# Two-layer hybrid decoder trunk: first weight tiles loaded in two pieces, angles computed early, k factors and k transposes moved, one output weight tile held back

## The reference, cut to what matters

```python
for layer in range(DEPTH):                       # DEPTH = 2
    if layer == 0:
        z = rms_norm(x, ab_norm_g) @ ab_w_in     # 512 pooling columns, 3 * 512 attention columns
        a = pool_mixer(z[..., :512], pool_w, pool_scale)
        b = diff_attention(z[..., 512:], cos, sin, ...)   # 4 heads, two softmax maps each, rotary on q and k
        x = x + concat([a, b]) @ ab_w_out
    else:
        z = rms_norm(x, ml_norm_g) @ ml_w_in     # q, k (short causal conv), v, output gate, gates
        h = rms_norm(mlstm_chunkwise(q, k, v, li, lf)) * sigmoid(o)   # 4 heads
        x = x + h @ ml_w_out
    x = x + conv_ffn(x, ...)                     # up 1024 -> 5632, causal conv, silu gate, down 2816 -> 1024
```

## Time and profile before

| | |
|---|---|
| median of 3 runs | 2274.3 us (2273.61 to 2274.34) |
| the profiled execution's own time | 2274.28 us |
| its span, first to last instruction | 2272.5 us |
| PE busy | 2261.0 us, 10747 matmuls |
| DVE, ACT, POOL busy | 1190.7, 572.2, 882.0 us |
| granted TensorE clock | 1.000 over the span |

### The profile page before, as it was taken

One profiled execution on the slowest core, in us unless ns is written; L12 is line 12 of the kernel. 1 busy time (PEld: TensorE's weight loads), 2 busy tenths in 40 slices (PEclk: granted clock), 3 DMA queues, 4 the chain that ended last, 5 costly groups with the idle time before them and its releaser, 6 DMA issues.

```text
span 2272.5 us, 27216 instructions
## 1 busy us (share of the span) xinstructions
PE 2261.0 (99%) x10747; PEld 1870.7 (82%) x10747; DVE 1190.7 (52%) x1176; ACT 572.2 (25%) x888; POOL 882.0 (39%) x395
## 2 busy tenths in 40 slices
PE   9999999999999999999999999999999999999999
PEld 7777778888888888888888898788888888888887
DVE  7776763464554555545644144444545555554554
ACT  5555441221111111111344333422111111111110
POOL 1212226444334433344643333275344433443342
PEclk9999999999999999999999999999999999999999
DMA  5111121111111111111321111031111111111111
GB/s 195 56 47 47 33 92 57 47 47 49 54 46 46 46 54 47 46 47 53 115 79 56 35 59 65 21 135 45 51 47 46 46 55 46 46 46 52 50 47 74
DMA packets 38721, 132.29 MB, mean 58 GB/s; under 512 B 4912, under 2 KB 6768, under 8 KB 38640
## 3 DMA queue, kind: packets, MB, share of 16 engines
q1 hardware_dynamic: 35760, 122.24, 16.7%
q10 hardware_dynamic: 2880, 8.91, 1.0%
HBM read 118.26 MB, written 8.68 MB: 56 GB/s over the span
## 4 chain that ended last, share of the span: by engine, by line
PE 95%; DVE 3%; issue 1%; ACT 0%; DMA 0%; SPq 0%; ACTq 0%; DVEq 0%
PE pj L1367 42%; PE dn L1387 17%; PE pj L347 15%; PE pj L325 6%; PE pj L1860 3%; PE dn L1438 3%; PE dn L686 1%; PE pj L712 1%; PE pj L1438 1%; PE pj L506 1%; PE pj L696 1%; PE dn L1998 1%; PE dn L2007 1%; PE dn L1886 1%; PE pj L1886 1%
## 5 line engine op out<-in xcount | busy, mean ns | idle before, releaser
L1661 POOL TENSOR_TENSOR w_hi<-w_raw,ones 128x1024 fp32r<-128x1024 f32 x186 | 356.0, 1914 | 1329.9 <-PE pj L1367 564.0
L1663 POOL TENSOR_TENSOR w_lo<-w_raw,w_hi 128x1024 fp32r<-128x1024 f32 x186 | 468.3, 2518 | 14.6
L1491 DVE SCALAR_TENSOR_TENSOR ffn_y<-ffn_h,params,ffn_y 128x1024 f32<-128x1024 f32 x176 | 323.6, 1838 | 117.6 <-ACT ffn_y L1499 109.0
L1499 ACT ACTIVATE ffn_y<-ffn_h,params 128x1024 f32<-128x1024 f32 x88 | 109.6, 1245 | 886.6 <-DVE ffn_h L1480 886.6
L1480 DVE TENSOR_TENSOR ffn_h<-pj,rms_bc 128x1024 f32<-128x1024 f32 x88 | 107.8, 1225 | 365.5 <-PE pj L1367 351.9
L1540 DVE TENSOR_TENSOR res<-dn,res 128x1024 f32<-128x1024 f32 x144 | 176.1, 1223 | 115.4 <-PE dn L1387 115.4
L1367 PE MATMUL pj<-xb_hi,w_hi 128*128 128x512 f32 x704 | 216.9, 389 | 0.0
L1367 PE MATMUL pj<-xa_hi,w_hi 128*128 128x512 f32 x704 | 216.9, 389 | 0.0
L1367 PE MATMUL pj<-xb_hi,w_lo 128*128 128x512 f32 x704 | 216.7, 389 | 0.0
L1367 PE MATMUL pj<-xa_hi,w_lo 128*128 128x512 f32 x704 | 216.7, 389 | 0.0
L1367 PE MATMUL pj<-xa_lo,w_hi 128*128 128x512 f32 x704 | 216.7, 389 | 0.0
(11 more groups left out here) (321 smaller groups left out, 3550.4 us busy)
## 6 DMA issues: line engine op xcount, KB each, us to landing
w_raw<-weights SPq DMA_DIRECT2D x189, 512.0 KB, 3.5
x_first<-x_t SPq DMA_DIRECT2D x8, 512.0 KB, 9.8
res<-x_t SPq DMA_DIRECT2D x8, 512.0 KB, 6.8
scratch<-res ACTq DMA_DIRECT2D x8, 512.0 KB, 2.6
res<-scratch SPq DMA_DIRECT2D x8, 512.0 KB, 8.4
y_t<-res ACTq DMA_DIRECT2D x7, 512.0 KB, 2.6
q_turned<-q_raw SPq DMA_DIRECT2D x16, 128.0 KB, 2.3
k_turned<-k_raw SPq DMA_DIRECT2D x16, 128.0 KB, 2.3
```

What stands on the lines that cost most here:

```text
L1491: dve.scalar_tensor_tensor(y[:, :], h[:, SH - lag:SH - lag + S], f.tap(j, m, q), y[:, :], ALU.mult, ALU.add).then_inc(taps[f.l], 1)
L1499: act.activation(f.y[m][:, :], f.h[m][:, SH:SH + S], ACT.Identity, bias=f.tap(j, m, 3), scale=f.tap(j, m, 2)).then_inc(center[f.l], 1)
L1661: pool.tensor_tensor(whi[:, w, :], raw[:, r, :], ones[:, 0:1].to_broadcast([P, D]), ALU.mult).then_inc(w_high, 1)
L1663: pool.tensor_tensor(wlo[:, w, :], raw[:, r, :], whi[:, w, :].bitcast(F32), ALU.subtract).then_inc(w_ready, 1)
```

## The change

It has four parts.

- **Opening.** Tiles 0 and 1 are loaded and split in two pieces, columns 0 to 383 (chunks 0 to 2, `FIRST` = 384) and the rest. SP's order is: first piece of tile 0, x 0 to 2, first piece of tile 1, rest of tile 0, x 3, rest of tile 1, x 4 to 7, constants. Parameters, positions and `inv_freq` are issued by ACT at its start. ACT makes `angle` and `turns_int` ahead of its first x chunk; DVE takes the turns off and folds once ahead of its first `xa_lo`, and folds again and clamps ahead of `xa_lo` 3. Squares get a second buffer (`sq_second`) for even chunks. The sines are taken after the last square, and their two stores are issued by SP instead of ACT. Warm-up matmuls are 384 columns wide. POOL also waits for the last sum of squares before its first split.
- **Key factors.** `dve_KB` half 0 moves from the start of block 7 to block 6, ahead of its combine.
- **Key transposes.** `pe_KT(0)` comes after G = 6 instead of G = 5.
- **Held tile.** POOL waits for six `cat_lo` of layer 1 before it splits tile T_OUT1+2.

```diff
@@ pe_group
-            if first:
+            if n in (0, 1):
+                if first:
+                    pe.wait_ge(first_ready, n + 1)
+                if k * P == FIRST:
+                    pe.wait_ge(w_ready, n + 1)
+            elif first:
                 pe.wait_ge(w_ready, n + 1)
                 pe_take(pe, j)
@@ act_norm_square (add_squares reads squares_of(ph, c) likewise)
+                ahead = 2 if ph == 0 else 1
+                if c > ahead:
+                    act.wait_ge(norm_acc[ph], c - ahead)
+                act.activation(squares_of(ph, c)[:, :], src, ACT.Square).then_inc(norm_sq[ph], 1)
@@ sp_tables
+            for t, table in enumerate((sinq, cosq)):
+                sp.wait_ge(tabs, t + 1)
+                sp.dma_start(scratch[t, :, 0:SQ], table[:, :]).then_inc(tab_out, 16)
@@ pe_mixer0
-            pe.wait_ge(w_high, 1)
+            pe.wait_ge(first_high, 1)
             for i in range(N_WARM[1]):
-                pe.matmul(dn[:, 1, 0:HALF], whi[:, 0, 0:P], whi[:, 0, 0:HALF], start=True, stop=True)
+                pe.matmul(dn[:, 1, 0:FIRST], whi[:, 0, 0:P], whi[:, 0, 0:FIRST], start=True, stop=True)
@@ new helpers (the rest cuts are the same from column FIRST, on w_in, w_high and w_ready)
+        def act_first_cut(act, n):
+            act.wait_ge(first_in[n], 16)
+            act.activation(whi[:, n, 0:FIRST], raw[:, n, 0:FIRST], ACT.Copy).then_inc(first_high, 1)
+        def dve_first_cut(dve, n):
+            dve.wait_ge(first_high, n + 1)
+            dve.tensor_tensor(wlo[:, n, 0:FIRST], raw[:, n, 0:FIRST], whi[:, n, 0:FIRST].bitcast(F32),
+                              ALU.subtract).then_inc(first_ready, 1)
@@ act_mixer0 (helpers high, square, sines, angles left out)
+            act.dma_start(par[:, 0:PC_FFN], params[:, 0:PC_FFN]).then_inc(s_par, 16)
+            act.dma_start(posi[:, :], pos_in).then_inc(s_pos, 16)
+            act.dma_start(invc[:, :], invf).then_inc(s_inv, 16)
             act_first_cut(act, 0)
...
+            angles()
             act.wait_ge(s_par, 16)
             act.wait_ge(set_dve, 4)
             for c in range(3):
                 high(c)
             act_first_cut(act, 1)
+            act_rest_cut(act, 0)
+            high(3)
+            act_rest_cut(act, 1)
+            high(4)
             square(0)
-            for c in range(3, KC):
+            square(1)
+            for c in range(5, KC):
                 high(c)
-                square(c - 2)
...
+                square(c - 3)
+            square(KC - 3)
             square(KC - 2)
-            act_first_cut(act, 2)
+            act_rest_cut(act, 2, 0)
             square(KC - 1)
...
+            sines()
             act_stat(act, 0)
@@ dve_mixer0
+            dve_turns_off(dve)
+            dve_fold(dve, ALU.is_gt, math.pi, -2 * math.pi)
             for c in range(3):
                 dve_norm(dve, 0, c, XA, xin[:, c, :])
             dve_first_cut(dve, 1)
...
+            dve_rest_cut(dve, 0)
             dve_fold(dve, ALU.is_lt, -math.pi, 2 * math.pi)
             dve_reduced(dve)
+            dve_norm(dve, 0, 3, XA, xin[:, 3, :])
+            dve_rest_cut(dve, 1)
+            dve_norm(dve, 0, 4, XA, xin[:, 4, :])
+            add_squares(dve, 0, 1)
+            for c in range(5, KC):
+                dve_norm(dve, 0, c, XA, xin[:, c, :])
+                add_squares(dve, 0, c - 3)
+            for c in range(KC - 3, KC):
+                add_squares(dve, 0, c)
+            dve_rest_cut(dve, 2, 0)
             dve_stat(dve, 0)
@@ dve_mixer0, heads
-                    if i == TB - 1 and not last:
-                        dve_KB(dve, h + 1, 0)
                     dve_mask(dve, h, i)
...
+                    if i == TB - 2 and not last:
+                        dve_KB(dve, h + 1, 0)
                     dve_combine(dve, h, i)
@@ pe_layer1
-                    if h == 0 and G == 5:
+                    if h == 0 and G == 6:
                         pe_KT(pe, 0)
@@ pool_layer1
+                if n == T_OUT1 + 2:
+                    pool.wait_ge(cat_lo[1], EARLY_CAT)
                 pool_cut(pool, n, n, 16 * (n // RAW_RING + 1))
@@ sync block
-            sp_load(sp, 0, 0)
-            sp.dma_start(par[:, 0:PC_FFN], params[:, 0:PC_FFN]).then_inc(s_par, 16)
+            sp_first_load(sp, 0)
             for c in range(3):
                 sp.dma_start(xin[:, c, :], x_in[c, :, :]).then_inc(s_xin[c], 16)
-            sp_load(sp, 1, 1)
+            sp_first_load(sp, 1)
+            sp_rest_load(sp, 0)
+            sp.dma_start(xin[:, 3, :], x_in[3, :, :]).then_inc(s_xin[3], 16)
+            sp_rest_load(sp, 1)
+            sp.dma_start(xin[:, 4, :], x_in[4, :, :]).then_inc(s_xin[4], 16)
@@ gpsimd block
             pool.wait_ge(set_dve, 4)
+            pool.wait_ge(norm_acc[0], KC - 1)
             pool.wait_ge(w_ready, 3)
```

More of the change, by code:

```diff
@@ L21 @@
 SQ = S // 4
+FIRST = 3 * P
 HEADS = 4
@@ L147, in program @@
         posi = at("pos_int", [P, SQ], I32, r_b + 8 * K4)
[L148 to L154, removed]
+        ang = at("angle", [P, SQ], F32, r_b + 8 * K4 + 1024)
+        turn = at("turns", [P, SQ], F32, r_b + 8 * K4 + 2048)
+        turni = at("turns_int", [P, SQ], I32, r_b + 8 * K4 + 3072)
+        red = at("angle_reduced", [P, SQ], F32, r_b + 9 * K4)
+        redc = at("angle_size", [P, SQ], F32, r_b + 9 * K4 + 1024)
+        sinq = at("sin_packed", [P, SQ], F32, r_b + 9 * K4 + 2048)
+        cosq = at("cos_packed", [P, SQ], F32, r_b + 9 * K4 + 3072)
+        sq2 = at("sq_second", [P, S], F32, r_b + 10 * K4)
         gq8 = small("q_gain_scaled", 1)
@@ L211, in program @@
         dn_free = [sem(f"dn_free{i}") for i in range(2)]
-        N_CONST = 5
+        N_CONST = 4
         s_const = sem("s_const")
         s_par = sem("s_par")
+        s_inv = sem("s_inv")
         s_xin = [sem(f"s_xin{c}") for c in range(KC)]
@@ L392, in act_norm_high, with squares_of @@
             act.activation(X[0][:, c, :], src, ACT.Copy, scale=pc(PC_NORM + ph * KC + c)).then_inc(xt_hi[ph], 1)
+        def squares_of(ph, c):
+            return sq2 if ph == 0 and c % 2 == 0 else sqt
         def act_norm_square(act, ph, c, src):
@@ L434, in program @@
         tab_in = sem("tab_in")
+        first_in = [sem(f"first_in{n}") for n in range(2)]
+        first_high = sem("first_high")
+        first_ready = sem("first_ready")
         angle_in = sem("angle_in")
@@ L958, in square, with sines, angles @@
                 act_norm_square(act, 0, c, xin[:, c, :])
+            def sines():
+                act.wait_ge(angle_in, 1)
+                act.activation(redc[:, :], red[:, :], ACT.Abs).then_inc(red_abs, 1)
+                act.activation(sinq[:, :], red[:, :], ACT.Sin).then_inc(tabs, 1)
+                act.wait_ge(red_abs, 1)
+                act.activation(cosq[:, :], redc[:, :], ACT.Sin, bias=halfpi[:, 0:1], scale=-1.0).then_inc(tabs, 1)
+            def angles():
+                act.wait_ge(s_pos, 16)
+                act.wait_ge(s_inv, 16)
+                act.activation(ang[:, :], posi[:, :], ACT.Copy, scale=invc[:, 0:1]).then_inc(turn_in, 1)
+                act.wait_ge(turn_in, 1)
+                act.activation(turni[:, :], ang[:, :], ACT.Copy, scale=1.0 / (2 * math.pi)).then_inc(turn_in, 1)
+            angles()
+            act.wait_ge(s_par, 16)
+            act.wait_ge(set_dve, 4)
             for c in range(3):
@@ L962, in act_mixer0 @@
             act_first_cut(act, 1)
+            act_rest_cut(act, 0)
+            high(3)
+            act_rest_cut(act, 1)
+            high(4)
             square(0)
-            for c in range(3, KC):
+            square(1)
+            for c in range(5, KC):
                 high(c)
-                square(c - 2)
[L967 to L971, removed]
+                square(c - 3)
+            square(KC - 3)
             square(KC - 2)
-            act_first_cut(act, 2)
+            act_rest_cut(act, 2, 0)
             square(KC - 1)
[L975 to L981, removed]
-                act.dma_start(scratch[t, :, 0:SQ], table[:, :]).then_inc(tab_out, 16)
+            sines()
             act_stat(act, 0)
@@ L1151, in dve_mixer0 @@
             dve_first_cut(dve, 1)
-            for c in range(3, KC):
-                dve_norm(dve, 0, c, XA, xin[:, c, :])
-                add_squares(dve, 0, c - 2)
-            dve_turns_off(dve)
-            add_squares(dve, 0, KC - 2)
-            dve_fold(dve, ALU.is_gt, math.pi, -2 * math.pi)
+            dve_rest_cut(dve, 0)
             dve_fold(dve, ALU.is_lt, -math.pi, 2 * math.pi)
             dve_reduced(dve)
-            add_squares(dve, 0, KC - 1)
-            dve_first_cut(dve, 2)
+            dve_norm(dve, 0, 3, XA, xin[:, 3, :])
[8 more added lines that the diff above has]
+            dve_rest_cut(dve, 2, 0)
             dve_stat(dve, 0)
```

22 lines of the change are left out of this document (10 added, 12 removed).

## The result

The changed kernel takes 2282.89 us (median of 6 runs, 2281.92 to 2283.70) against 2274.06 us before (6 runs, 2273.61 to 2274.34): ratio 1.0040, 95% interval 1.0030 to 1.0049. It is slower by about 8.8 us, outside my range, by more than the 0.2% that a measurement can tell. The profiled execution took 2282.88 us, 8.60 more than the one of before.

The account below looks back on a forecast made before the run. PE was taken as the bound, busy 2261.0 of 2272.5 us. 2274.28 - 0.35 (opening) + 0 (key factors) + 0.75 (key transposes) + 2.0 (held tile) = 2276.7 us; own range 2275.3 to 2278.0, 8 in 10 within 2273.2 to 2278.3.

Parts of the forecast that it names:

- L: Opening: time at which positions and `inv_freq` have landed; forecast 5.0, with 4 to 6.5 in the forecast's range.
- E: Opening: end of DVE's first `xa_lo`, forecast at the later of 9.6 and 10.0 us.
- E + 21.9: Opening: time at which PE ends before the statistics of layer 0, forecast as 31.9 us.
- The rival of the late angles: Opening: positions and `inv_freq` land late, L tending to 12.0; 2279.8 us at L = 8.5; chance 0.08.
- PE waiting some 4 us at line 1840: End of head 3: sign expected in the changed profile, PE waiting for `m_num` before its transposes; loss forecast 2.0 us.
- -0.35: Opening: forecast gain of 0.35 us, statistics starting at 31.9 or 32.0 instead of 32.3.
- The stall of 0.9 us before `xa_lo` 3: Opening: PE, four groups done, waits 0.9 us for `xa_lo` 3, which the old order didn't have.
- E + 6.4: Opening: forecast time at which DVE is through `xa_lo` 3, after splits, a fold and the clamp.
- The 0.06 for slower by over 0.2%: Whole kernel: chance given to a total above 2278.8 us, by late angles in the opening.
- the hold's 1.7: End of head 3: low end, in us, of the held tile's loss in the forecast's own range.
- the hold's 2.4: End of head 3: upper bound, in us, of the held tile's loss, forecast as 2.0.

Follow-up runs that it names:

- the filler: Changed kernel plus 16 matmuls of the constant ones on PE, ahead of its wait for the last `m_num` at the end of head 3: 2280.91 us.

## Why the prediction was wrong, step by step

- **The step that failed: "Issued third at about 1.6, L is 5.0."** It landed at 8.70. I took the duration of one row, the parameters' 3.4 us, for the third transfer of a queue, so the time of the two ahead of it was left out. In both orders that were run the third lands at 8.4 to 8.7, whichever it is. In the trace before, `inv_freq` took 10.0 us from issue behind SP's full queue, like its neighbours, which tells nothing of its own price; the bounds were 2.3 and 10.4 us, and I kept only L from 4 to 6.5 in the forecast's range. The rest of the formula held: E = L + 4.6 gives 13.3, and `xa_lo` ended at 13.29. (The terms named for it add up to 4.3 only; in the trace the steps take 4.27 and the gaps between them the other 0.3.) With the transfer removed, PE's part (E + 21.9 forecast) was 31.76 - 10.22 = 21.5. The rival of the late angles had the right consequence, at a chance of 0.08, and gave 2279.8 for L = 8.5. Its reason, small transfers served behind SP's chunks with L towards 12.0, is not what the runs show: the wait was for places in ACT's own queue.
- **A missing step: the clock.** No term of the sum had it. In the opening it cost (36.30 - 13.29) - 21.5 = 1.5 us, and 2.6 by the same sum in the run with `inv_freq` first. At head 3 I forecast "PE waiting some 4 us at line 1840" and priced only the wait; the transposes and the next groups at 0.50 cost 8.54 - 6.19 = 2.35 us more by the traces (8.54 is the loss once PE is back at full clock), 2.0 by the medians with the filler. The opening thus went -0.35 + 3.3 (E at 13.3 instead of 10.0) + 1.5 - 0.4 (21.5 instead of 21.9) = 4.0, of which 3.6 is left at the second mark.
- **Right, held tile.** POOL's start: 1464.1 forecast, 1468.37 - 4.31 (the loss by then) = 1464.06. `m_num` starts 5.84 us after it (5.87 forecast), and the wait costs 1.88 (2.0 forecast).
- **Right, key transposes.** 0.75 forecast, 4.31 - 3.6 = 0.7 in the change, 0.7 alone by the medians.
- **Right, key factors.** 0 forecast; the wait moved to line 696 (line 715 after), three times 0.5 us, as its row in the list of waits shows.
- **Small misses that cost nothing.** x chunk 0 landed at about 5.5, not 7.3 (its shortest landing was 4.3 us from issue); E hung on L. The stall of 0.9 us before `xa_lo` 3 came to some 0.15 where the frequencies are in the parameters (PE at 16.05 instead of 15.90): DVE was through at E + 5.8, not E + 6.4.
- **The sum, mended:** 2274.28 + 3.6 + 0 + 0.7 + 1.9 + 2.35 = 2282.8, against 2282.88.
- **The chances.** Two errors of the same sign, both at places where I had already forecast an idle PE. The 0.06 for slower by over 0.2% rested on L alone. The hold's wait was a sure loss in my text, and what follows a wait was not asked. The forecast's own range of 2275.3 to 2278.0 doesn't follow from the bounds named for it either: the hold's 1.7 and L up to 5.4 give 2276.4, L = 6.5 and the hold's 2.4 give 2278.2. The measured time lies outside both.

## What to carry to other kernels

Give a transfer that an engine waits for its place in its queue and not only its size: here the third place cost 2.4 us more than the second for 128 KB and 3.0 for 512 bytes. A table of 4 bytes a row that goes along in a larger transfer of as many rows saves that place; with the clock that it had cost, this was worth 4.9 us. When a step is held back to spare one engine, look for what it will run beside at its new time, and hold it to behind the last small step on the path. A new wait of PE can have a second price, the matmuls behind it at half clock: 1.5 us behind the wait of 2.96 here and 2.35 behind the one of 3.98.

## What the runs showed of the hardware that I had not expected

- **A third transfer cost ACT's queue 2.4 to 3.0 us beside a full SP queue, whatever its size.** `inv_freq` as third landed 3.0 us after positions (8.70 and 5.70); as first it put parameters and positions off by 2.5 and 2.7, and positions as third landed 2.4 after the second. One transfer is 144 packets (3024 less 2880). The rule that I cited from the Trainium skill, DMA: Bandwidth & Descriptors, "Queues, rings and completion order" (turns between queues), held in so far as ACT's data weren't put behind SP's backlog, which took 8.4 us. Why the packets take that long, and whether they would beside an idle SP queue, no run here shows.
- **The clock fell in PE's idle times of 2.96 and 3.98 us**, in the middle of dense work at head 3, and stayed at 1.00 behind those of 0.97, 1.12 and 1.3 us. The length of one wait doesn't decide it: with `inv_freq` first it stayed at 1.00 behind 3.23 us and fell in a wait of 1.25 us that came 1.2 us later. Matmul pairs went from 0.62 to 1.05 us, and in the change it took until about 17.2 and 1481.5 us to come back. Both levels only, as the Trainium skill, TensorE: Matmul & The Clock Gate, "Part 1: The HAM clock gate (the "warmup" mystery)", has it; the windows show 0.50 and 1.00 with mixed values only where it changed.
- **The old opening itself moves by 0.6 us** from one trace to another (PE goes on at 14.29 or 13.69) with the landings.
